# Order of TensorE's down-projections among the rounds of a pair of expert groups

## The chip, the cores and the metric

The kernel runs as one launch on one core of one Trainium2 chip. The metric is the device time in microseconds of that core, from launch to end; lower is better. The profile is one execution of the same program, recorded by the hardware. Its times count from the start of the span, the stretch from the core's first to its last instruction.

## The reference, cut to what matters

The whole program is a float32 transformer on 256 tokens of width 1024: two layers of one kind, then two of a second kind. The last layer ends in a mixture of experts, and only that part is touched here:

```
def moe_swiglu(x, w_router, w_gate, w_up, w_down):
    logits = (x @ w_router).astype(jnp.float32)
    top_val, top_idx = lax.top_k(logits, TOP_K)          # TOP_K = 2 of N_EXPERTS = 8
    top_w = jax.nn.softmax(top_val, axis=-1)
    gate = jnp.einsum('bsk,bske->bse', top_w, one_hot(top_idx, N_EXPERTS)).astype(x.dtype)
    y = jnp.zeros_like(x)
    for e in range(N_EXPERTS):
        h = jax.nn.silu(x @ w_gate[e]) * (x @ w_up[e])   # 1024 -> D_FF_EXPERT = 3584
        y = y + gate[..., e:e + 1] * (h @ w_down[e])     # 3584 -> 1024
    return y
```

Each expert has three weight matrices of 14.7 MB in float32, so the eight experts together have 352 MB that must come in from memory once.

## The kernel before, in words

**Which tokens.** For each expert the tokens that chose it are gathered into 96 slots (FIRST = 96, three tiles of 32). The function `first_slots` computes all eight experts for these slots; a later loop for experts with more than 96 tokens runs only if one has them.

**Groups and pairs.** The hidden width 3584 of an expert is cut in 7 groups of 512, so there are 56 groups in all, and `first_slots` takes them two at a time: 28 pairs, `q` = 0 to 27, with the groups `i0 = 2q` and `i1 = 2q + 1`, and a last turn `q` = 28 that only finishes. A group has three weight blocks of 2 MB: gate, up and down. The six blocks of a turn are loaded by SyncE (SP) in the order gate i0, up i0, down i0-2, gate i1, up i1, down i1-2, into a ring of six buffers. Load n may start when load n-6 is used, and SP waits for these one after the other in the order of the loads.

**Rounds.** The weights stream through TensorE (PE) while three 32-slot tiles of tokens are held, and four such 32-column tiles run side by side in the array. A pair has 2 groups x 2 matrices x 3 tiles = 12 products, which makes three rounds of four (`tiles`, L1248), 64 matmuls each. Round 1 writes a bank of ring "d" and is the last user of gate i0. Round 2 writes the other bank of "d", is the last user of up i0 and the first of gate i1. Round 3 writes a bank of ring "s" and is the last user of gate i1 and up i1.

**From rounds to the hidden values.** ScalarE (ACT) applies silu to the gate parts (L1633 to L1649) and VectorE (DVE) multiplies them by the up parts (L2265 to L2277). Rounds 1 and 2 give the half `hid_a`; round 3 gives the rest: ACT L1649, then DVE L2276 and L2277, which mark `hid_b`. Then PE turns the hidden values (`turn_hidden`): it waits for `hid_a`, makes four transposes (L1294), waits for `hid_b`, makes four more (L1300). ACT copies both to SBUF (L1656).

**Downs.** `down(i)` multiplies the turned hidden values of group i by its down block (48 matmuls, L1275 and L1281) and adds up over the 7 groups of the expert in two banks of ring "x". In turn q PE does the downs of the pair before, `i0-2` and `i1-2`. After an expert's seventh group ACT and DVE take the result away (`outcome`: ACT L1623, DVE L2232 to L2237), `scatter` spreads it back over the tokens (PE L1232, after round 1 of some turns) and DVE adds it up (`gather_out`, L2247). At three turns PE also gathers the tokens of two more experts (L1210) and turns their weights (L1221), both after round 2.

**What sets the order.** All of it is written out by hand, for each engine on its own: PE's loop at L1300 to L1331, ACT's at L1625 to L1658, DVE's at L2250 to L2281. Each engine executes in its own order, and an instruction that waits holds up everything behind it. The weights' order is set by the plan's loop over `gate_up` and `lower`.

Of the kernel before, what the change touches and what calls it, by code (L numbers as in the profile page):

```python
# [452 lines left out]
def build(nc, a, out, book, cut=None):  # L453
# [15 lines left out]
    with ExitStack() as ctx:  # L469
# [362 lines left out]
        def _(pe):  # L832
# [403 lines left out]
            def first_slots(groups):  # L1236

                per = len(groups) // EXPERTS
                x_of = [xs[i // per // 2 % 2][:, :, i // per % 2 * FIRST:(i // per % 2 + 1) * FIRST] for i in range(len(groups))]

                def tiles(r, parts, release):

                    views = {w: slot(w) for _, w, _ in parts}
                    b, n = bank(lane, r)
                    pe.wait_ge(*emptied(lane, r, n))
                    for k in range(KD):
                        for j, (i, w, c) in enumerate(parts):
                            last = pe.matmul(b[TILE * j:TILE * j + TILE, :], x_of[i][:, k, TILE * c:TILE * c + TILE],  # L1248
                                             views[w][:, k, :], start=(k == 0), stop=(k == KD - 1))
                    last.then_inc(*lane.tick(filled[r], ("full", r, n), *[("used", w) for w in release]))  # L1250

                accs = None

                def down(i):

                    nonlocal accs
                    at = i % per
                    if at == 0:
                        accs = [bank(lane, "x") for _ in range(2)]
                        for _, n in accs:  # L1260
                            pe.wait_ge(*emptied(lane, "x", n))
                    (b0, n0), (b1, n1) = accs
                    v = slot(groups[i]["down"])
                    pe.wait_ge(*lane.of(("hid_turned", i // 2)))

                    def mine(f, c):

                        turned, at = ((hid_a, (3, 0, 1)), (hid_b, (2, 3, 0)))[i % 2]
                        return turned[:, f, TILE * at[c]:TILE * at[c] + TILE]

                    for f in (0, 2):
                        first, final = at == 0 and f == 0, at == per - 1 and f == 2
                        for o in range(2):
                            for j, (c, half) in enumerate(((0, 0), (1, 0), (2, 0), (2, 1))):
                                last = pe.matmul(b0[TILE * j:TILE * j + TILE, :], mine(f + o, c),  # L1275
                                                 v[:, f + o, 512 * half:512 * half + 512], start=(first and o == 0),
                                                 stop=(final and o == 1))
                        if final:
                            last.then_inc(*lane.tick(x_full, ("full", "x", n0)))
                        for j, (c, o) in enumerate(((0, 0), (1, 0), (0, 1), (1, 1))):  # L1280
                            last = pe.matmul(b1[TILE * j:TILE * j + TILE, :], mine(f + o, c), v[:, f + o, 512:1024],  # L1281
                                             start=first, stop=final)
                    if at < per - 1:
                        last.then_inc(*lane.tick(down_done, ("e_down", i), ("used", groups[i]["down"])))
                    else:
                        last.then_inc(*lane.tick(x_full, ("full", "x", n1), ("e_down", i), ("used", groups[i]["down"])))

                def turn_hidden(q):

                    pe.wait_ge(*lane.of(("hid_a", q)))  # L1290
                    b, n = bank(lane, "a")
                    pe.wait_ge(*emptied(lane, "a", n))
                    for f in range(4):
                        last = pe.transpose(b[:, f * P:(f + 1) * P], hidden[:, 0, f * P:(f + 1) * P], ident[:, :])  # L1294
                    last.then_inc(*lane.tick(a_full, ("full", "a", n)))
                    pe.wait_ge(*lane.of(("hid_b", q)))
                    b, n = bank(lane, "a")
                    pe.wait_ge(*emptied(lane, "a", n))
                    for f in range(4):
                        last = pe.transpose(b[:, f * P:(f + 1) * P], hidden[:, 1, f * P:(f + 1) * P], ident[:, :])  # L1300
                    last.then_inc(*lane.tick(a_full, ("full", "a", n), ("hid_read", q)))

                gather(0)
                pairs = len(groups) // 2
                for q in range(pairs + 1):
                    i0, i1 = 2 * q, 2 * q + 1
                    if q < pairs:
                        g0, g1 = groups[i0], groups[i1]
                        pe.wait_ge(*lane.of(("xg", i0 // per // 2 * 2)))
                        tiles("d", [(i0, g0["gate"], 1), (i0, g0["gate"], 2), (i0, g0["gate"], 0), (i0, g0["up"], 0)],  # L1310
                              [g0["gate"]])
                    for m in scattered_at(q, per):
                        scatter(m)
                    if q < pairs:
                        pe.wait_ge(*lane.of(("xg", i1 // per // 2 * 2)))
                        tiles("d", [(i0, g0["up"], 1), (i0, g0["up"], 2), (i1, g1["gate"], 0), (i1, g1["gate"], 1)],
                              [g0["up"]])
                    for g in gathered_at(q, per):
                        gather(g)
                    for g in [0] if q == 0 else gathered_at(q, per):  # L1320
                        turn_weights(g)
                    if q:
                        down(i0 - 2)
                    if q < pairs:
                        tiles("s", [(i1, g1["up"], 2), (i1, g1["gate"], 2), (i1, g1["up"], 0), (i1, g1["up"], 1)],
                              [g1["gate"], g1["up"]])
                    if q:
                        down(i1 - 2)
                    if q < pairs:
                        turn_hidden(q)  # L1330
                scatter(EXPERTS - 1)  # L1331
                state["pass"], state["e_group"] = EXPERTS, len(groups)
# [122 lines left out]
        def _(act):  # L1455
# [169 lines left out]
            def first_slots(groups):  # L1625
# [3 lines left out]
                for q in range(pairs):  # L1629
# [3 lines left out]
                        act.wait_ge(*lane.of(("hid_b", q - 1)))  # L1633
                    act.activation(gated[96:P, 0, :], b[64:96, :], ACT.Silu).then_inc(*lane.tick(act_order, ("silu_0", q)))
                    act.activation(gated[0:64, 0, :], b[0:64, :], ACT.Silu).then_inc(*lane.tick(act_order))
                    b, n = bank(lane, "d")
                    act.wait_ge(*lane.of(("full", "d", n)))
                    act.activation(gated[64:P, 1, :], b[64:P, :], ACT.Silu).then_inc(*lane.tick(act_order, ("silu_1", q)))  # L1638
# [3 lines left out]
                        weights_turned(g)  # L1642
                    for _ in range(scattered_banks(q, per)):
                        bank(lane, "s")
                    if ended_at(2 * q - 2, per):
                        outcome((2 * q - 2) // per)
                    b, n = bank(lane, "s")
                    act.wait_ge(*lane.of(("full", "s", n)))
                    act.activation(gated[0:32, 1, :], b[32:64, :], ACT.Silu).then_inc(  # L1649
                        *lane.tick(act_order, ("silu_2", q)))  # L1650
                    if ended_at(2 * q - 1, per):
                        outcome((2 * q - 1) // per)
                    for dst in (hid_a, hid_b):
                        b, n = bank(lane, "a")
                        act.wait_ge(*lane.of(("full", "a", n)))
# [122 lines left out]
        def _(dve):  # L1778
# [471 lines left out]
            def first_slots(groups):  # L2250
# [3 lines left out]
                for q in range(pairs + 1):  # L2254
# [3 lines left out]
                    for g in gathered_at(q, per):  # L2258
                        picks(g)
                        weights(g)  # L2260
                    if q < pairs:
                        if q:
                            dve.wait_ge(*lane.of(("hid_read", q - 1)))
                        b, n = bank(lane, "d")
                        dve.wait_ge(*lane.of(("silu_1", q)))  # L2265
                        post(dve.tensor_tensor(hidden[96:P, 0, :], gated[96:P, 0, :], b[96:P, :], ALU.mult),  # L2266
                             ("free", "d", n), sem=d_free)
                        b, n = bank(lane, "d")
                        post(dve.tensor_tensor(hidden[0:64, 0, :], gated[0:64, 0, :], b[0:64, :], ALU.mult),
                             ("free", "d", n), ("hid_a", q), sem=d_free)  # L2270
                    if ended_at(i0 - 2, per):
                        outcome((i0 - 2) // per)
                    if q < pairs:
                        b, n = bank(lane, "s")
                        dve.wait_ge(*lane.of(("silu_2", q)))
                        post(dve.tensor_tensor(hidden[64:P, 1, :], gated[64:P, 1, :], b[64:P, :], ALU.mult))  # L2276
                        post(dve.tensor_tensor(hidden[0:32, 1, :], gated[0:32, 1, :], b[0:32, :], ALU.mult),  # L2277
                             ("free", "s", n), ("hid_b", q), ("e_hidden", i0), ("e_hidden", i1), sem=s_free)
                    if ended_at(i1 - 2, per):
                        outcome((i1 - 2) // per)  # L2280
                gather_out(EXPERTS - 1)  # L2281
                state["pass"], state["e_group"] = EXPERTS, len(groups)

# [148 lines left out]
```

## Time and profile before

| what | value |
|---|---|
| median of 3 runs | 2592.01 us (2587.98 to 2606.04) |
| the profiled execution | 2597.7 us |
| its span | 2595.8 us |
| TensorE busy | 2450.5 us, 94% of the span |
| VectorE, ScalarE busy | 485.5 us, 401.8 us |
| HBM read | 556.49 MB |

The profiled execution is 5.7 us longer than the median of the runs, and lies inside their range; 1.9 us of it lie around the span. In the page's strips one digit is a slice of 64.9 us. Busy times of different engines overlap and don't add up to the span. The tiles in the profile are named by the buffers that the kernel reuses: `hT` and `N` hold gathered tokens in this stage, `proj` holds the hidden values before and after ACT and DVE, `PT` the turned hidden values, `slots` the weight ring.

### The profile page before, as it was taken

Reading aid. Unit: us, or ns where it says so; the run is one execution under the profiler, and the core shown is the slowest. Engines: PE = TensorE matmul, PEld = TensorE weight load, DVE = VectorE, ACT = ScalarE, POOL = GpSimd, SP = SyncE. Lnnn points to the kernel's source line nnn. Section 1 sums busy time; section 2 is a strip of 40 time slices with the busy share of each in tenths; the row PEclk is TensorE's granted clock in tenths of the full one; section 3 lists DMA queues with packets and bytes.
Section 4 is the critical chain, followed back from the end, with each engine's and each line's share of the span. In section 5 each row is a group of like instructions: output and inputs, shape, how many; then the busy total and the mean of one; then the engine's idle time right before and its main releaser. Section 6 shows DMA issues by size and latency. Waiting matters only on the chain.

```text
span 2595.8 us, 33681 instructions
## 1 busy us (share of the span) xinstructions
PE 2450.5 (94%) x14810; PEld 1328.2 (51%) x14810; DVE 485.5 (19%) x1214; ACT 401.8 (15%) x970; POOL 109.0 (4%) x186
## 2 busy tenths in 40 slices
PE   7999999999999599999987897999999999999997
PEld 3678765578765264776647645333333333333332
DVE  3240003340001431200111623001011110111012
ACT  1330001330001151200010612110111111111101
POOL 2210100000000020000000200000000000000000
PEclk9899999999999779999995898999999999999999
DMA  9557634624333244243334223799999999999994
GB/s 291 182 54 184 222 114 141 219 86 151 130 122 131 96 138 148 105 158 133 134 98 146 74 102 120 264 391 373 358 369 390 373 357 370 392 336 370 390 372 165
DMA packets 247460, 567.89 MB, mean 219 GB/s; under 512 B 10224, under 2 KB 25776, under 8 KB 247312
## 3 DMA queue, kind: packets, MB, share of 16 engines
q1 hardware_dynamic: 235424, 532.24, 56.2%
q0 software_dynamic: 11888, 33.46, 5.9%
q8 instruction: 120, 1.97, 0.3%
q14 instruction: 28, 0.23, 0.0%
HBM read 556.49 MB, written 9.18 MB: 218 GB/s over the span
## 4 chain that ended last, share of the span: by engine, by line
PE 92%; DVE 4%; ACT 3%; issue 1%; DMA 1%; DVEq 0%; SPq 0%; ACTq 0%; POOLq 0%
PE ps_d L1248 15%; PE ps_a L874 12%; PE ps_x L1275 7%; PE ps_s L1248 7%; PE ps_a L1061 7%; PE ps_d L1061 7%; PE ps_x L1078 4%; PE ps_s L1078 4%; PE ps_x L1281 4%; PE ps_x L981 3%; PE ps_s L916 3%; PE ps_x L916 3%; PE ps_a L1045 2%; PE ps_a L963 2%; PE ps_d L1045 2%; PE ps_s L1232 1%
## 5 line engine op out<-in xcount | busy, mean ns | idle before, releaser
L874 PE MATMUL ps_a<-slots,hT 128*128 128x512 f32 (+4 forms) x672 | 275.2, 568 | 14.2 <-ACT hT L1485 9.9
L1275 PE MATMUL ps_x<-slots,PT 128*32 128x512 f32 x1792 | 212.9, 592 | 0.8 <-ACT PT L1656 0.8
L874 PEld LDWEIGHTS ps_a<-slots,hT 128*128 128x128 f32 x672 | 126.6, 195 | 156.0 <-issue 140.9
L1248 PE MATMUL ps_d<-slots,hT 128*32 128x512 f32 x1792 | 195.8, 593 | 0.6 <-ACT hT L1606 0.6
L1248 PE MATMUL ps_d<-slots,N 128*32 128x512 f32 x1792 | 196.0, 593 | 0.0
L1061 PE MATMUL ps_a<-hT,slots 128*128 128x256 f32 x864 | 192.7, 381 | 2.5 <-issue 2.5
L1061 PE MATMUL ps_d<-hT,slots 128*128 128x256 f32 x864 | 190.9, 379 | 0.0
L1061 PEld LDWEIGHTS ps_a<-hT,slots 128*128 128x128 f32 x864 | 165.0, 191 | 30.6 <-issue 8.5
L1061 PEld LDWEIGHTS ps_d<-hT,slots 128*128 128x128 f32 x864 | 164.2, 190 | 22.3
L2330 DVE TENSOR_TENSOR proj<-proj,ps_d 128x512 f32<-128x512 f32 x33 | 22.7, 688 | 597.7 <-PE ps_d L1061 523.7
L1275 PEld LDWEIGHTS ps_x<-slots,PT 128*32 128x32 f32 x1792 | 58.2, 110 | 132.9 <-issue 132.9
L1248 PEld LDWEIGHTS ps_d<-slots,hT 128*32 128x32 f32 x1792 | 56.4, 110 | 129.2 <-issue 128.4
L1248 PEld LDWEIGHTS ps_d<-slots,N 128*32 128x32 f32 x1792 | 56.3, 110 | 128.8 <-issue 128.8
L1078 PE MATMUL ps_x<-slots,proj 128*128 128x512 f32 x264 | 121.6, 592 | 0.0
L1078 PE MATMUL ps_s<-slots,proj 128*128 128x512 f32 x264 | 121.6, 592 | 0.0
L1281 PE MATMUL ps_x<-slots,PT 128*32 128x512 f32 x896 | 116.7, 592 | 0.0
L1600 ACT ACTIVATE proj<-ps_a 128x512 f32<-128x512 f32 x33 | 19.7, 597 | 543.6 <-PE ps_a L1061 516.0
L2266 DVE TENSOR_TENSOR proj<-proj,ps_d 32x512 f32<-32x512 f32 x28 | 19.4, 694 | 437.9 <-ACT proj L1638 437.9
L1248 PE MATMUL ps_s<-slots,hT 128*32 128x512 f32 x896 | 98.7, 592 | 0.0
L1248 PE MATMUL ps_s<-slots,N 128*32 128x512 f32 x896 | 98.7, 592 | 0.0
L1078 PEld LDWEIGHTS ps_x<-slots,proj 128*128 128x128 f32 x264 | 50.2, 190 | 63.1 <-issue 63.1
L1078 PEld LDWEIGHTS ps_s<-slots,proj 128*128 128x128 f32 x264 | 50.2, 190 | 56.7 <-issue 56.0
(346 smaller groups left out, 2362.7 us busy)
## 6 DMA issues: line engine op xcount, KB each, us to landing
slots<-in_moe_w_gate SPq DMA_DIRECT2D x56, 2048.0 KB, 9.8
slots<-in_moe_w_up SPq DMA_DIRECT2D x56, 2048.0 KB, 11.1
slots<-in_moe_w_down SPq DMA_DIRECT2D x56, 2048.0 KB, 12.0
slots<-in_ffn_w_gate_up SPq DMA_DIRECT2D x20, 2048.0 KB, 9.3
slots<-in_ffn_w_down SPq DMA_DIRECT2D x10, 2048.0 KB, 8.4
slots<-in_w_in SPq DMA_DIRECT2D x8, 2048.0 KB, 9.6
slots<-in_ff_w_gate SPq DMA_DIRECT2D x5, 2048.0 KB, 7.8
slots<-in_ff_w_up SPq DMA_DIRECT2D x5, 2048.0 KB, 7.7
```

The source lines that it names most:

```text
L874: last = pe.matmul(b[:, 0:c], lhs[:, k, t * P:(t + 1) * P], v[:, k, :], start=(k == 0), stop=(k == s["k"] - 1))
L916: last = pe.matmul(b[:, :], hT[:, k, t * P:(t + 1) * P], v[:, k, :], start=(k == ks[0]), stop=(k == ks[-1]))
L963: last = pe.transpose(b[:, at * P:(at + 1) * P], PR[:, u % 2, j, t, kc * P:(kc + 1) * P], ident[:, :])
L981: last = pe.matmul(b[:, o:o + dv], PT[:, u % 2, j, turned_at[kc, t], :], named[name][:, kc, c:c + dv], start=(kc == kcs[0]), stop=(kc == k ...
L1045: last = pe.matmul(b[:, f * S + t * P:f * S + (t + 1) * P], v[:, k, (f0 + f) * P:(f0 + f + 1) * P], hT[:, k, t * P:(t + 1) * P], start=(k ...
L1061: last = pe.matmul(b[:, f * S:(f + 1) * S], v[:, k, (f0 + f) * P:(f0 + f + 1) * P], hT[:, k, :], start=(k == 0), stop=(k == KD - 1))
L1078: last = pe.matmul(b[:, :], hid[:, n_group % 2, f, t * P:(t + 1) * P], v[:, f, half * 512:(half + 1) * 512], start=start, stop=stop)
L1232: pe.matmul(b[:, :], gives[:, m // 2 % 2, m % 2, t * P:(t + 1) * P], y_e[0:FIRST, 512 * half:512 * half + 512], start=True, stop=True).the ...
L1248: last = pe.matmul(b[TILE * j:TILE * j + TILE, :], x_of[i][:, k, TILE * c:TILE * c + TILE], views[w][:, k, :], start=(k == 0), stop=(k == ...
L1275: last = pe.matmul(b0[TILE * j:TILE * j + TILE, :], mine(f + o, c), v[:, f + o, 512 * half:512 * half + 512], start=(first and o == 0), st ...
L1281: last = pe.matmul(b1[TILE * j:TILE * j + TILE, :], mine(f + o, c), v[:, f + o, 512:1024], start=first, stop=final)
L2330: dve.tensor_tensor(hid[:, n_group % 2, f0:f0 + 2, :].rearrange("p f s -> p (f s)"), silu[:, p % 2, :], b[:, :], ALU.mult).then_inc(*lane. ...
```

## The change

Within a turn PE's order is changed. Written without the scatters and gathers, it was

```
round 1, round 2, down(i0-2), round 3, down(i1-2), turn_hidden
```

and it becomes

```
round 1, down(i0-2), round 2, down(i1-2), round 3, turn_hidden
```

ACT and DVE take away an expert's result (`outcome`) correspondingly earlier in their own order. The order of the loads is not changed, nor is any instruction's shape.

```diff
@@ PE, first_slots
                     for m in scattered_at(q, per):
                         scatter(m)
+                    if q:
+                        down(i0 - 2)
                     if q < pairs:
                         ...
                     for g in [0] if q == 0 else gathered_at(q, per):
                         turn_weights(g)
                     if q:
-                        down(i0 - 2)
+                        down(i1 - 2)
                     if q < pairs:
                         tiles("s", [(i1, g1["up"], 2), (i1, g1["gate"], 2), (i1, g1["up"], 0), (i1, g1["up"], 1)],
                               [g1["gate"], g1["up"]])
-                    if q:
-                        down(i1 - 2)
                     if q < pairs:
                         turn_hidden(q)
@@ ACT, first_slots
                     act.activation(gated[0:64, 0, :], b[0:64, :], ACT.Silu).then_inc(*lane.tick(act_order))
+                    if ended_at(2 * q - 2, per):
+                        outcome((2 * q - 2) // per)
                     b, n = bank(lane, "d")
                     ...
-                    if ended_at(2 * q - 2, per):
-                        outcome((2 * q - 2) // per)
+                    if ended_at(2 * q - 1, per):
+                        outcome((2 * q - 1) // per)
                     b, n = bank(lane, "s")
                     act.wait_ge(*lane.of(("full", "s", n)))
                     act.activation(gated[0:32, 1, :], b[32:64, :], ACT.Silu).then_inc(
                         *lane.tick(act_order, ("silu_2", q)))
-                    if ended_at(2 * q - 1, per):
-                        outcome((2 * q - 1) // per)
@@ DVE, first_slots
+                    if ended_at(i0 - 2, per):
+                        outcome((i0 - 2) // per)
                     if q < pairs:
                         ...
-                    if ended_at(i0 - 2, per):
-                        outcome((i0 - 2) // per)
+                    if ended_at(i1 - 2, per):
+                        outcome((i1 - 2) // per)
                     if q < pairs:
                         b, n = bank(lane, "s")
                         ...
-                    if ended_at(i1 - 2, per):
-                        outcome((i1 - 2) // per)
```

## Rows read from the trace of the kernel before

**Rows 1.** The page: busy by engine; strips of PE's clock and of DMA.
```profile
PE 2450.5 (94%) x14810; PEld 1328.2 (51%) x14810; DVE 485.5 (19%) x1214; ACT 401.8 (15%) x970; POOL 109.0 (4%) x186
...
PEclk9899999999999779999995898999999999999999
DMA  9557634624333244243334223799999999999994
```

**Rows 2.** Groups of PE in 1653.4:2560: busy, mean ns, idle before.
```profile
L1275 PE MATMUL ps_x<-slots,PT 128*32 128x512 f32 x1600 | 190.0, 592 | 0.0
...
L1300 PE MATMUL ps_a<-ident,proj 128*128 128x128 f32 x102 | 15.4, 273 | 0.0
```

**Rows 3.** Timeline of PE, turn q = 4: start, us, work, xcount.
```profile
1749.66 13.94 PE L1248 MATMUL ps_d<-slots,hT 128*32 128x512 f32 x128
1763.42 1.90 PE L1275 MATMUL ps_x<-slots,PT 128*32 128x512 f32 x16
...
1768.57 7.05 PE L1248 MATMUL ps_s<-slots,hT 128*32 128x512 f32 x64
1775.43 1.90 PE L1275 MATMUL ps_x<-slots,PT 128*32 128x512 f32 x16
...
1780.70 0.65 PE L1294 MATMUL ps_a<-ident,proj 128*128 128x128 f32 x4
...
1781.72 7.07 PE L1248 MATMUL ps_d<-slots,hT 128*32 128x512 f32 x64
```

**Rows 4.** Timeline of all engines at the end of turn q = 0.
```profile
1643.67 7.07 PE L1248 MATMUL ps_s<-slots,hT 128*32 128x512 f32 x64
...
1650.68 0.65 PE L1294 MATMUL ps_a<-ident,proj 128*128 128x128 f32 x4
...
1650.81 0.59 ACT L1649 ACTIVATE proj<-ps_s 32x512 f32<-32x512 f32 x1 [6.37 <-PE ps_s L1248]
...
1651.43 0.69 DVE L2276 TENSOR_TENSOR proj<-proj,ps_s 64x512 f32<-64x512 f32 x1 [6.07 <-ACT proj L1649]
1652.16 0.68 DVE L2277 TENSOR_TENSOR proj<-proj,ps_s 32x512 f32<-32x512 f32 x1
...
1652.89 0.66 PE L1300 MATMUL ps_a<-ident,proj 128*128 128x128 f32 x4 [1.56 <-DVE proj L2277]
1653.47 1.92 PE L1248 MATMUL ps_d<-slots,hT 128*32 128x512 f32 x16
```

**Rows 5.** Waits in 1660:2580: us in total, times, longest.
```profile
ACT proj L1649 <- PE ps_s L1248: 288.3, 27, 11.6
...
PEld ps_s L1232 <- DVE O L2247: 9.9, 15, 0.8
```

**Rows 6.** Timeline of SP (weight loads) in turn q = 4.
```profile
1743.62 0.37 SPq L660 DMA_DIRECT2D slots<-in_moe_w_gate  x1
...
1768.81 0.37 SPq L660 DMA_DIRECT2D slots<-in_moe_w_down  x1
```

**Rows 7.** DMA issues in 1743:1749: KB, us from issue to landing.
```profile
slots<-in_moe_w_gate SPq DMA_DIRECT2D x1, 2048.0 KB, 10.1
...
slots<-in_moe_w_down SPq DMA_DIRECT2D x1, 2048.0 KB, 15.5
```

**Rows 8.** The same in 1756:1769, of three loads the last.
```profile
slots<-in_moe_w_down SPq DMA_DIRECT2D x1, 2048.0 KB, 11.3
```

**Rows 9.** The same in 1599:1601, with no other load on the way.
```profile
slots<-in_moe_w_gate SPq DMA_DIRECT2D x1, 2048.0 KB, 7.9
```

**Rows 10.** Window with the pause of turn q = 0: length, busy (PE, PEld, DVE, ACT, POOL), clock, DMA.
```profile
1650.00:1660.00 10.00, 8.44 (x80) 2.88 (x76) 1.37 (x2) 1.78 (x3) 0.00 (x0) 1.00 0.85 311
```

**Rows 11.** Windows after a wait of 5.44 us of PE, before the experts.
```profile
1622.00:1624.00 2.00, 2.00 (x8) 2.00 (x7) 0.00 (x0) 0.00 (x0) 0.00 (x0) 0.50 0.04 8
1624.00:1626.00 2.00, 2.00 (x11) 2.00 (x10) 0.00 (x0) 0.49 (x1) 0.00 (x0) 0.74 0.00 0
```

**Rows 12.** Timeline of PE there: the gather of the first two experts.
```profile
1621.45 7.20 PE L1210 MATMUL ps_a<-proj,X 128*128 128x192 f32 x32 [5.44 <-DVE O L2204]
```

## The prediction, made before the change was run

> **What bounds the kernel now.** I read four views, from coarse to fine. The page first: TensorE (PE) is busy for 94% of the span, and in the last 14 slices, where the experts lie, it runs at a clock of 9 tenths or more while the DMA strip shows nines too [rows 1]. So two resources are near full there. The groups of PE over the experts say which one sets the pace: from 1653.4 to 2560 us not one group has idle time before it, the transposes L1300 and the downs L1275 included [rows 2]. Nothing PE waits for comes late. What is gained on another engine, or by an earlier transfer, is worth nothing here; the only thing that can change the time is a gap between PE's instructions.
>
> The timeline of one turn gives the parts [rows 3]. Rounds 1 and 2 start at 1749.66 and the first down at 1763.42, so a round is 6.88 us; the next starts give down 5.15 (1763.42 to 1768.57) and round 3 6.86 (1768.57 to 1775.43). The turn ends when the next one's round 1 starts, at 1781.72: 32.06 us. I use 6.87 for a round. From the start of the second down (1775.43 + 5.15 = 1780.58) to the next turn there are 1.14 us, the two sets of transposes with a small gap ahead of them.
>
> **What the second down does there now.** It stands between round 3 and the transposes, and round 3's results need time: ACT must apply silu, DVE must multiply twice, and only then may PE do L1300. The first turn, q = 0, has no downs, so it is exactly the end of a turn that the change makes everywhere: round 3, then the transposes at once. There the chain is bare [rows 4]: round 3 starts at 1643.67, the first transposes at 1650.68, ACT at 1650.81, DVE at 1651.43 and 1652.16, and L1300 at 1652.89 after 1.56 us of idle PE, released by DVE L2277. The next round 1 starts at 1653.47, 9.80 us after round 3 began.
>
> **The sum, part by part.**
> - Down i0-2 moves ahead of round 2. It needs `hid_turned` of the turn before, which ACT copies out after L1300, about 0.6 us a copy by the like of ACT L1649 [rows 4]; round 1 with 6.87 us still lies between. Nothing for its wait. Without round 1 ahead of it the wait would show, but that is so in turn 28 alone, before and after alike.
> - Down i1-2 moves ahead of round 3. Both moves leave 48 matmuls of 5.15 us as they are, and rows 3 show no gap at the borders of round and down (starts 6.87 and 5.15 apart). Nothing for the move itself.
> - The end of a turn. Before: round 3, down, 1.14, so 6.87 + 5.15 + 1.14 = 13.16 us (1768.57 to 1781.72). After: down 5.15, then the pattern of q = 0 with 9.80, so 14.95 us. The difference is **1.79 us** per turn. Turns with downs and transposes are q = 1 to 27; ACT L1649 and PE met 27 times in this view [rows 5]. 27 x 1.79 = **48.3 us**. From below, the idle time alone, 1.56, would give 42.1 us. From above, if L1294 were not hidden in the wait either (it lasts 0.65 with its tail, 0.5 by the starts), 2.28 would give 61.6 us. I take 1.79, since it is the measured distance of the same instructions in the same order at the same clock.
> - Can ACT or DVE be late for this chain? Both idle until round 3 ends: ACT L1649 waited 288.3 us in 27 times on PE, 10.7 us each [rows 5]. Their new work ahead of it, `outcome`, now belongs to a down that ended a whole round (6.87 us) before. Four short instructions of about 0.7 us each fit in it. Nothing.
> - The banks of ring "x". When an expert ends on i0-2, down i1-2 starts the next expert and must find both banks empty. Round 3 covered that before, round 2 does now, with the same 6.87 us. Nothing; bare, it would be those same 2.8 us, four times.
> - Scatters stay after round 1 and gathers after round 2, with the same neighbours ahead. Scatter's short waits on DVE, 9.9 us in 15 times [rows 5], stay.
> - The loads. SP's queue is passed in the old order, but the buffers come free in another one. Count from the start of round 1. Before: gate i0 at 6.87, up i0 13.74, down 18.9, gate i1 and up i1 25.8, down 30.9. After: gate i0 6.87, up i0 and the down (freed earlier, but behind it in SP's order) 18.9, and gate i1, up i1 and the second down all at 30.9. What does a load take? From the landing of the gate issued at 1743.62 (+10.1 = 1753.7) to that of the down issued at 1768.81 (+11.3 = 1780.1) five more loads land in 26.4 us, 5.28 each; alone, a load takes 7.9 [rows 6 to 9], so 2.6 us pass before its bytes flow. After: three loads issued at 30.9 land at 38.8, 44.1 and 49.3. They are needed one turn (33.85 us) later: gate i1 at 45.9, up i1 at 57.9, the down at 52.7. The next gate i0 and up i0 land at 54.6 and 60.5 and are needed at 67.7, the first down at 65.8 for 74.6. The smallest reserve is **3.4 us**, of down i1-2. Before it was about 2.8, of gate i1 (landed 1753.7, needed at 1749.66 + 6.87 = 1756.5), and no wait came of it. The six loads fill 31.7 us of a turn that is now 33.85. Nothing, as a reserve of that size held before.
>
> The sum: 2597.7 + 48.3 = 2646.0 us for an execution like the profiled one, whose span would be 2644. The median of the runs lies 5.7 us under the profiled execution, so I forecast 2592.0 + 48.3 = **2640 us**, 1.9% slower. There is no term on the other side, since PE had no idle time to win back.
>
> **The clock.** In the window with the pause of q = 0 PE was busy 8.44 of 10 us and the granted clock was 1.00, that is 2.4 GHz [rows 10]. The new pauses are of that size, one per 33.85 us. The Trainium skill (TensorE: Matmul & The Clock Gate, section "A second HAM failure mode: psum-queue depth-cycling") says that short idle times between groups of matmuls, when frequent, can make the clock swing between its two levels. The one pause here speaks against it; 27 in a row have not been seen.
>
> **The rivals.**
> 1. *The clock falls at each pause* (chance 0.05). After a wait of 5.44 us the first gather began at 1621.45 [rows 12], at a granted clock of 0.50; the window 1624 to 1626 has 0.74, about the middle [rows 11], so some 3.5 us ran at 1.2 GHz, of which half, 1.8 us, is lost. At all 27 pauses: 47 us more, 2687 us. For it: many pauses, and ring banks in turn; against: rows 10.
> 2. *Weights come late* (0.06). Three loads now leave together, and the last has three services ahead of its need. It decides once that load takes over 21.8 us from issue instead of the 18.4 worked out; the longest of rows 7 is 15.5, with two in front of it. Every microsecond over that stalls PE before round 3's down, in 27 turns: at one over, 2667 us. In PE's waits L1275 would then stand behind a DMA.
> 3. *Not slower: the chain hides* (0.05). If L1300 finds `hid_b` ready sooner than in q = 0, say because ACT and DVE answer round 3 faster in the steady turns, the pause shrinks. The point at which it decides is 0.96 us per turn (26 / 27): below it the change is within 1%. At no pause at all and with scatter's waits gone too, which now meet other neighbours, the time is 2592.0 - 9.9 = 2582 us; with the pause at half, 2616 us. Against it: ACT started 0.13 us after PE's next instruction and DVE 0.03 us after ACT ended in q = 0 [rows 4], so nothing in the chain but work is left.
> 4. *The change does not do what it says* (0.02): a wait hidden in semaphore values keeps PE's order in effect, 2592 us. PE executes in its written order, so this is nearly excluded.
>
> The forecast itself has the remaining 0.82. Its own range is 2592 + 42 = 2634 to 2592 + 62 = 2654, and medians of three runs here spread by some microseconds (runs from 2588 to 2606), so 2628 to 2658. Reaching a little into rivals 2 and 3 gives 2622 to 2662, which leaves out less than 2 in 10. A measurement of this kernel tells about 1% (26 us) from no change. Slower by over 1%: forecast, rivals 1 and 2, 0.93, less a little for a pause near 1 us, 0.91. Within 1%: 0.08. Faster by over 1%: 0.01, as nothing idle is there to be won.
>
> **What would show it.** PE's group L1300 with about 42 us of idle before it in 27 to 28 waits, each near 1.56, released by DVE L2277; starts of round 1 33.85 us apart in plain turns; the ACT wait for round 3 unchanged in kind; down groups L1275 with no idle; a clock of 1.00 from 1700 on; DMA at a mean some 5% lower over the experts (31.7 of 33.85). It would be wrong if L1275 or L1248 wait for a DMA (rival 2), if the clock strip shows less than nines (rival 1), or if L1300's idle is well under 26 us in all (rival 3).

## The result, and the profile after

The changed kernel takes 2646.97 us in the median of 4 runs (2633.74 to 2660.04), the kernel before 2599.03 us in its 4 (2587.98 to 2611.62). The ratio is 1.0183, with a 95% interval of 1.0095 to 1.027. In a second set, 6 runs against 17, it is 1.0194 (1.0153 to 1.0235). The change makes the kernel slower by 1.8 to 1.9%; 1.9% was forecast.

Single executions of either kernel differ by 25 us, half of the effect, so I measure the part that the change touches by itself: from the start of the first gather (L1210) to the start of the last scatter (L1232), called "the stage" below. In the kernel before it began at 1621.45 [rows 12]. Its end in the kernel before, in the timeline of PE:

```profile
2577.64 3.86 PE L1232 MATMUL ps_s<-proj,PR 96*128 96x512 f32 x8 [1.49 <-issue]
```

Both ends in the changed kernel, in the same view:

```profile
1609.47 2.90 PE L1210 MATMUL ps_a<-proj,X 128*128 128x192 f32 x8 [5.44 <-DVE O L2204]
...
2613.69 3.86 PE L1232 MATMUL ps_s<-proj,PR 96*128 96x512 f32 x8 [1.49 <-issue]
```

The stage takes 956.2 us before and 1004.2 after: **48.0 us more**, where 48.3 were worked out. Two lines of the page of the changed kernel answer to [rows 1]; the clock is at nines in the experts' slices as before, and PE has lost a little of its share:

```profile
PE 2445.6 (93%) x14810; PEld 1318.3 (50%) x14810; DVE 484.2 (18%) x1214; ACT 403.9 (15%) x970; POOL 108.8 (4%) x186
...
PEclk9999999999999699999976998999999999999999
```

Where the idle time is, the groups of PE over the experts say (1653.4:2590; columns as in [rows 2]):

```profile
L1275 PE MATMUL ps_x<-slots,PT 128*32 128x512 f32 x1696 | 201.6, 593 | 0.0
...
L1300 PE MATMUL ps_a<-ident,proj 128*128 128x128 f32 x104 | 17.1, 287 | 40.4 <-DVE proj L2279 40.4
```

One group alone has any, L1300, and its releaser is DVE L2279, the multiply that was L2277 [rows 2, 4]. The window leaves out the pause of turn 0 and that of turn 27, so these are 26 of the 28. The DMA share over 1700 to 2500 us has a mean of 0.95 in windows of 100 us, where it was 1.00, the 5% less that was named as a sign. One turn in the timeline of PE (against [rows 3]):

```profile
1733.44 7.05 PE L1248 MATMUL ps_s<-slots,hT 128*32 128x512 f32 x64
1740.42 0.66 PE L1294 MATMUL ps_a<-ident,proj 128*128 128x128 f32 x4
1742.63 0.66 PE L1300 MATMUL ps_a<-ident,proj 128*128 128x128 f32 x4 [1.55 <-DVE proj L2279]
1743.22 7.07 PE L1248 MATMUL ps_d<-slots,hT 128*32 128x512 f32 x64
1750.11 1.90 PE L1275 MATMUL ps_x<-slots,PT 128*32 128x512 f32 x16
...
1762.12 1.90 PE L1275 MATMUL ps_x<-slots,PT 128*32 128x512 f32 x16
```

Round 3 to the next round 1 is 9.78 us (turn 0 had 9.80), and the next round 1 starts at 1777.05, 33.83 us after this one's 1743.22, against 32.06 before. In the chain of waits one such pause reads, in order of time (start, us, what):

```profile
1706.72 0.60 ACT proj L1651
1707.32 0.02 issue
1707.35 0.69 DVE proj L2278
1708.04 0.03 issue
1708.07 0.69 DVE proj L2279
1708.76 0.04 issue
1708.80 0.66 PE ps_a L1300 x4
```

Round 3's last matmul is done at 1706.70. Silu and two multiplies, 2.0 us of work with 0.1 us between them: there is nothing in the chain but work. In every turn with rounds the end has become what the end of turn 0 was [rows 4].

### The profile page after: what moved, and what is told of

Same layout as the page of the kernel before. It is cut to its first block, busy times and chain, and to the rows that moved or that the text cites. A ratio compares the mean times of both kernels' runs of the same rounds, so it can differ in the third digit from the quotient of the medians.

```text
span 2631.9 us, 33681 instructions
## 1 busy us (share of the span) xinstructions
PE 2445.6 (93%) x14810; PEld 1318.3 (50%) x14810; DVE 484.2 (18%) x1214; ACT 403.9 (15%) x970; POOL 108.8 (4%) x186
## 4 chain that ended last, share of the span: by engine, by line
PE 90%; DVE 5%; ACT 3%; issue 1%; DMA 1%; DVEq 0%; SPq 0%; ACTq 0%; POOLq 0%
PE ps_d L1248 15%; PE ps_a L874 12%; PE ps_x L1275 7%; PE ps_s L1248 7%; PE ps_a L1061 7%; PE ps_d L1061 7%; PE ps_x L1078 4%; PE ps_s L1078 4%; PE ps_x L1281 4%; PE ps_x L981 3%; PE ps_s L916 3%; PE ps_x L916 3%; PE ps_a L1045 2%; PE ps_d L1045 2%; PE ps_a L963 2%
```

## The experiments

In every table "stage" is first gather to last scatter in the profiled execution, and the ratio is to the kernel before, with its 95% interval. The changed kernel's two profiles agree within 0.2 us in the stage, which is what makes effects of a few microseconds readable at all.

| kernel | stage, us | ratio |
|---|---|---|
| before | 956.2 | 1 |
| changed | 1004.2 | 1.0183 (1.0095 to 1.027) |
| after_again: changed, once more | 1004.0 | 1.0194 (1.0153 to 1.0235) |
| first_down_only | 956.4 | 1.0011 (0.9982 to 1.0041) |
| second_down_only | 1011.5 | 1.0216 (1.0172 to 1.0259) |
| turn_b_late | 988.8 | 1.0131 (1.0089 to 1.0172) |
| shorter_chain | 986.6 | 1.0126 (1.0070 to 1.0182) |
| longer_chain | 1041.2 | 1.0313 (1.0257 to 1.0369) |
| slightly_longer | 1023.5 | 1.0275 (1.0231 to 1.0318) |
| longer_chain_before | 956.9 | 1.0006 (0.9976 to 1.0037) |
| after_loads | 1004.0 | 1.0176 (1.0133 to 1.0219) |
| turn_b_later | 963.6 | 1.0036 (1.0005 to 1.0067) |
| turn_b_later_loads | 963.4 | 1.0043 (1.0017 to 1.0069) |

**The same kernel again.**

> The changed kernel once more, timed in more rounds. From its first gather to its last scatter it took 1004.2 us, the kernel before 956.2 us. Bare chain at the end of a turn: the expert stage is again 1004 us within 1 us, some 48 us over before, ratio near 1.018. Late weights: the stage may vary by several us between executions, since memory does. Clock falling at the pauses: a granted clock under 1.00 in some windows of the experts, and a stage that varies. Any difference between executions that all three leave over must lie ahead of the experts.

The stage is 1004.0 us. The span of this execution was 2656.7 us, 24.8 more than in the profile above, and all of it lies ahead of the stage: its first gather starts at 1634.5 instead of 1609.5. The last section says what it is.

**Each move alone.** The first move by itself:

```diff
 round 1
+down(i0 - 2)
 round 2
-down(i0 - 2)
 round 3
 down(i1 - 2)
 turn_hidden(q)
```

> Only the first move: round 1, down i0-2, round 2, round 3, down i1-2, transposes. Bare chain: the second down stands between round 3 and the transposes again, so the whole loss goes: stage 956 us, the time of before, ratio 1.000 within 0.4%; PE's L1300 idle in turn 0 alone, 1.6 us. Late weights: the buffers of up i0 and down i0-2 still come free together, only gate i1, up i1 and down i1-2 don't, so a part of the loss stays if loads in bunches are its cause (10 to 30 us). Clock: no pauses, no loss.

The stage is 956.4 us, the time of before. PE's waits in it are those of before, the pause of turn 0 and two at the very end (engine, line, releaser, us in total, times, longest):

```profile
PE ps_a L1300 <- DVE proj L2277: 1.6, 1, 1.6
PE ps_s L1232 <- issue: 1.5, 1, 1.5
PE ps_x L1275 <- ACT PT L1656: 0.8, 1, 0.8
```

The second move by itself:

```diff
 round 1
 round 2
 down(i0 - 2)
+down(i1 - 2)
 round 3
-down(i1 - 2)
 turn_hidden(q)
```

> Only the second move: round 1, round 2, down i0-2, down i1-2, round 3, transposes. Bare chain: the 48 us are all there, since nothing stands between round 3 and the transposes. And a second price shows four times (turns 4, 11, 18, 25, where an expert ends on down i0-2): down i1-2 must now wait until the result of the last expert has left both banks, some 2 to 2.8 us each, 8 to 11 us in all. So a stage of about 1013 us, ratio 1.021. Late weights: the three loads at the end of a turn leave together as in the changed kernel, so about 1004 as well; only the waits in the profile, on DVE and not on a DMA, tell that apart.

1011.5 us. The pauses belong to the second move. And the second price is there, in the waits of PE (1640 to 2610 us, which leaves out the 28th pause):

```profile
PE ps_a L1300 <- DVE proj L2278: 41.9, 27, 1.6
PE ps_x L1275 <- DVE proj L2236: 6.0, 4, 1.5
```

L2236 is the last step of `outcome`. It came up 4 times and the stage is 1011.5 - 1004.2 = 7.3 us longer, 1.8 each, a little under the 8 to 11 expected. In the changed kernel round 2 stands there, and PE's waits have no such line.

**The chain covered, all else as changed.** The transposes of hid_b move behind the next round 1:

```diff
 round 1
+turn_b(q - 1)        # L1300's transposes and ACT's copy
 down(i0 - 2)
 round 2
 down(i1 - 2)
 round 3
-turn_hidden(q)
+turn_a(q)            # L1294's transposes and ACT's copy
```

> The changed order, but the second set of transposes (of hid_b, L1300) and its copy on ScalarE are put behind round 1 of the next turn. Rounds, downs and all releases of weights stay in the changed order, in bunches. Bare chain: 6.9 us of round 1 cover it, the pauses go, and the stage is back at 956 to 961 us (up to 0.15 us per turn more for one more border between transposes and matmuls), ratio 1.000 to 1.002. Late weights: the bunches stay and a turn has less time, so if they cost the 48 us, the stage stays near 1004 and L1275 or L1248 wait for a DMA. Clock: no pauses, no loss.

This missed: 988.8 us, not 956 to 961. The old pause is gone, and there is a new one, again bare, because the down waits for ACT's copy of what has just been turned (in the seven turns that are not counted a scatter stands between):

```profile
PE ps_x L1275 <- ACT PT L1638: 26.9, 21, 1.3
```

I had counted the cover of the first link, transposes after multiply, and not of the next, down after copy. Here no DMA is among the waits either, though the releases of the weights are in bunches as in the changed kernel. The next version puts a down between:

```diff
 round 1
+down(i0 - 2)         # waits for hid_a's copy only
 turn_b(q - 1)
-down(i0 - 2)
 round 2
 down(i1 - 2)         # waits for hid_b's copy
```

> The changed order with the transposes of hid_b behind down i0-2 of the next turn, which needs hid_a alone; down i0-2 waits for hid_a's copy only, down i1-2 for hid_b's. Round 1 and the down cover the chain to the transposes, round 2 covers ScalarE's copy, which stood bare (1.3 us, 20 to 21 times) when the transposes came right before the down. Bare chain: no pause is left, a stage of 956 to 960 us, ratio 1.000 to 1.003. Late weights: a turn has only some 32.2 us now and the load of down i1-2 landed 19.8 us after the end of round 3, while it is needed after 0.6 + 6.9 + 5.15 + 0.6 + 6.9 = 20.1 us. This rival is alive here for the first time: some turns may wait for a DMA at L1275, 0 to 0.5 us each, up to 10 us.

963.6 us: of the 48.0 us, 40.6 are gone. What is left is in the timeline of PE for one turn:

```profile
1698.55 7.05 PE L1248 MATMUL ps_s<-slots,hT 128*32 128x512 f32 x64
1705.53 0.66 PE L1294 MATMUL ps_a<-ident,proj 128*128 128x128 f32 x4
1706.12 7.07 PE L1248 MATMUL ps_d<-slots,hT 128*32 128x512 f32 x64
...
1718.27 0.66 PE L1303 MATMUL ps_a<-ident,proj 128*128 128x128 f32 x4
1718.86 7.07 PE L1248 MATMUL ps_d<-slots,hT 128*32 128x512 f32 x64
```

Each set of four transposes now costs 0.59 us and 0.11 us at its border (1705.53 less 1698.55 is 6.98, not 6.87). That is 1.40 us for both sets, where the two side by side took 1.14. The whole turn is some 32.35 us, 0.29 more than 32.06. 27 x 0.29 = 7.8, less 1.6 of turn 0, plus 0.8 for a second wait at the end, are 7.0 of the 7.4 us that are left. The 0.12 to 0.15 us that my expectations allow for the border was too small. PEld also showed a wait for weights, of which the next section tells.

**Late weights.** The changed kernel with the loads in the order in which the buffers come free:

```diff
-gate i0, up i0, down i0-2, gate i1, up i1, down i1-2
+gate i0, down i0-2, up i0, down i1-2, gate i1, up i1
```

> The changed kernel with the six loads of a turn in the order in which its buffers come free: gate i0, down i0-2, up i0, down i1-2, gate i1, up i1. No three loads leave together any more, and every block lands at least 5 us ahead of its use. Bare chain: the time is that of the changed kernel, stage 1004 us, ratio 1.018 to 1.019, pauses of L1300 unchanged. Late weights: were the bunched loads the cause of any of the 48 us, that part comes back and the stage is shorter than 1004.

1004.0 us, with PE pausing ahead of L1303 (the line that is L1300 elsewhere) for 43.5 us in 28 times. The order of the loads has no part in the loss. Yet the reserve in the changed kernel was thinner than I had worked out. The three loads that leave together, in the timeline of SP, and what they took from issue to landing (window 1735:1745 of the DMA view):

```profile
1740.55 0.37 SPq L660 DMA_DIRECT2D slots<-in_moe_w_gate  x1
1740.96 0.58 SPq L660 DMA_DIRECT2D slots<-in_moe_w_up  x1
1741.59 3.94 SPq L660 DMA_DIRECT2D slots<-in_moe_w_down  x1
```
```profile
slots<-in_moe_w_gate SPq DMA_DIRECT2D x1, 2048.0 KB, 9.2
slots<-in_moe_w_up SPq DMA_DIRECT2D x1, 2048.0 KB, 14.2
slots<-in_moe_w_down SPq DMA_DIRECT2D x1, 2048.0 KB, 18.7
```

The third landed at 1741.59 + 18.7 = 1760.3 and was needed at 1762.12: 1.8 us of reserve where 3.4 were forecast. In the split version, whose turn is shorter, this became a wait of PEld, the weight loads of PE (first fence), and with the new load order it went (second fence, all that PEld waits for there but issue):

```profile
PEld ps_x L1275 <- DMA slots<-in_moe_w_down: 5.3, 12, 0.6
```
```profile
PEld ps_s L1235 <- DVE O L2261: 10.5, 16, 0.8
```

> The split transposes (hid_b's behind down i0-2 of the next turn) together with the load order of the buffers' release. In the split version alone the stage was 963.6 us: 956.2, and 5.3 us in 12 waits for the down weights, and about 27 x 0.12 us for one more border between transposes and matmuls, less 1.6 us of turn 0. Late weights explain the 5.3 us and no more: with the new load order they go, and the stage is 958 to 959 us. If those waits had another cause they stay. The ratio to the kernel before is then 1.002, or 1.000 where ours can't be told apart.

The wait went, and the time did not: 963.4 us against 963.6. So those 5.3 us had cost nothing that shows. They stand in PEld's table and not in PE's: the load of the next weights waited up to 0.6 us while the matmuls before it still ran. The sum that gave them 5 us was wrong, and the borders above take that place.

**The length of the chain.** VectorE's first multiply of round 3 reads only what the silu of round 2 wrote, so it need not wait for `silu_2`, the silu of round 3:

```diff
-dve.wait_ge(*lane.of(("silu_2", q)))
+dve.wait_ge(*lane.of(("full", "s", n)))
 post(dve.tensor_tensor(hidden[64:P, 1, :], gated[64:P, 1, :], b[64:P, :], ALU.mult))
+dve.wait_ge(*lane.of(("silu_2", q)))
 post(dve.tensor_tensor(hidden[0:32, 1, :], ...
```

> The changed kernel, but VectorE's first multiply of round 3, which does not read what ScalarE's silu L1651 writes, waits for round 3 alone and not for that silu; only the second multiply waits for it. Silu (0.59 us) and first multiply (0.69) then run side by side. Bare chain: it is shorter by about 0.6 us in each of 28 turns, 15 to 18 us less than the changed kernel, a stage of about 987 to 989 us, ratio near 1.012. If the two engines hinder each other at the same bank, less is won. Late weights: down i1-2 had 1.6 to 2.1 us of reserve in the changed kernel, so its weights could just begin to be late; by that rival nothing is won.

986.6 us, 17.6 less than the changed kernel, 0.63 us per turn. The timeline shows silu and multiply starting together and the pause down from 1.55 to 0.93 us; both engines at one bank did not slow either:

```profile
1704.09 0.59 ACT L1651 ACTIVATE proj<-ps_s 32x512 f32<-32x512 f32 x1 [11.42 <-PE ps_s L1248]
1704.09 0.69 DVE L2278 TENSOR_TENSOR proj<-proj,ps_s 64x512 f32<-64x512 f32 x1 [9.92 <-PE ps_s L1248]
...
1705.54 0.66 PE L1300 MATMUL ps_a<-ident,proj 128*128 128x128 f32 x4 [0.93 <-DVE proj L2280]
```

The other way, with that multiply done twice:

```diff
 post(dve.tensor_tensor(hidden[64:P, 1, :], gated[64:P, 1, :], b[64:P, :], ALU.mult))
+dve.wait_ge(*lane.own())
+post(dve.tensor_tensor(hidden[64:P, 1, :], gated[64:P, 1, :], b[64:P, :], ALU.mult))
```

> The changed kernel with VectorE's first multiply of round 3 (64x512, 0.69 us) done twice, the second time after waiting for the first: the chain from round 3 to the transposes L1300 is longer by one such instruction and a wait. Bare chain: every added nanosecond shows in each of the 28 turns, 0.69 to 0.75 us x 28 = 19 to 21 us over the changed kernel, so a stage (first gather to last scatter) of 1024 us against 1004.2, and L1300's mean pause 2.3 us instead of 1.55. Late weights or a clock that falls: VectorE's work doesn't enter, no more than 1 or 2 us; a longer pause would even give the weights more time.

1041.2 us, 37.0 more than the changed kernel, nearly twice what every theory of mine said. The pause itself grew as it should, from 43.5 to 63.8 us in 28 times, 20.3 us. The rest is the clock. The windows around the end of one such pause, at 1722.67 (columns as in [rows 10]), and the group of rounds 1 and 2 in one half of the experts:

```profile
1722.00:1724.00 2.00, 1.33 (x12) 0.71 (x16) 0.61 (x1) 0.60 (x1) 0.00 (x0) 1.00 1.04 401
1724.00:1726.00 2.00, 2.00 (x15) 0.47 (x11) 0.00 (x0) 0.00 (x0) 0.00 (x0) 0.50 1.05 403
1726.00:1728.00 2.00, 2.00 (x19) 0.55 (x15) 0.00 (x0) 0.00 (x0) 0.00 (x0) 0.64 1.05 387
1728.00:1730.00 2.00, 2.00 (x24) 0.64 (x20) 0.00 (x0) 0.00 (x0) 0.00 (x0) 1.00 1.05 387
```
```profile
L1248 PE MATMUL ps_d<-slots,N 128*32 128x512 f32 x1792 | 205.6, 613 | 0.0
```

The granted clock is 0.50 soon after the pause and 1.00 again by 1728; the group's mean is 613 ns where it was 593 in the changed kernel. By the starts of the matmuls, 9 of the 27 rounds 1 that follow a pause are longer, eight by 1.70 us and one by 1.15, with 0.45 more in the transposes just ahead of it. The down that follows the 28th pause is longer by 1.70 too. Together 16.9 us, which with the 20.3 makes 37.2, 0.2 over the 37.0: the first gather was that much shorter. Is there a pause in between at which this begins? A repeat of 192 instead of 512 columns:

> The changed kernel with a small repeat of VectorE's first multiply (64x192, about 0.3 us) in the chain, between the changed kernel (pause 1.55 us, stage 1004 us, clock 1.00) and the one with the whole repeat (pause 2.27 us, stage 1041 us). The whole repeat cost 37 us: 20 us of pause and some 17 us in which the granted clock was at 0.5 after a pause. By pause alone this one costs 28 x 0.35 = 10 us, stage 1014 us, clock 1.00 among the experts. If the clock falls after pauses of 1.9 us too, the stage is longer by up to another 17 us and round 1's matmuls have a mean above 593 ns.

1023.5 us, 19.3 more than the changed kernel, with pauses of 1.94 us. After 5 of the 28 pauses the clock fell: 4 rounds 1 are longer, and the down behind the last pause. One of the rounds, in the timeline of PE, takes 8.77 us instead of 7.07 (first fence). The down's first 16 matmuls take 2.85 us, where they take 1.92 in the changed kernel (second and third fence):

```profile
1976.75 0.66 PE L1300 MATMUL ps_a<-ident,proj 128*128 128x128 f32 x4 [1.94 <-DVE proj L2281]
1977.33 8.77 PE L1248 MATMUL ps_d<-slots,N 128*32 128x512 f32 x64
```
```profile
2632.73 2.85 PE L1275 MATMUL ps_x<-slots,PT 128*32 128x512 f32 x16 [0.78 <-ACT PT L1656]
```
```profile
2601.69 1.92 PE L1275 MATMUL ps_x<-slots,PT 128*32 128x512 f32 x16 [0.78 <-ACT PT L1656]
```

Five times 1.7 are 8.5 us, and 28 x 0.39 us of longer pause are 10.9, together the 19.3 within 0.1. At pauses of 1.55 us, in the changed kernel, its repetition and the one with the other load order, no round 1 of 81 is longer, nor is the down behind the last pause. What makes the clock fall at one pause and not at the next was not tested, and each of the longer chains was profiled once.

**The control: the longer chain in the old order.** The same doubled multiply in the kernel before:

> The kernel before with the same doubled multiply (0.69 us and a wait) in VectorE's part of round 3. Bare chain: here down i1-2 (5.15 us) covers the chain, which grows from 2.1 to 2.8 us, so only turn 0, which has no down, is longer: stage 956.2 + 0.7 = 956.9 us, ratio 1.000. If VectorE's work cost time in another way (SBUF or PSUM traffic beside TensorE), the stage would grow by up to 20 us as well.

956.9 us: 0.7 more, all of it in turn 0. The instruction that cost 37.0 us in the one order costs 0.7 in the other.

## Why the prediction was right

- *No idle time of PE to win.* Right: first_down_only, which changes nothing but the place of one down and its `outcome`, neither wins nor loses anything (956.4 against 956.2 us).
- *1.79 us per turn, 48.3 us in all, from turn 0's bare chain.* Right to 0.3 us: 48.0 in the stage, 1.77 by the turns' starts (33.83 less 32.06). That it is this chain is shown from both sides: 0.63 us off it moves the stage by 28 times as much, 0.73 us on it lengthens the pauses 28 times, and the same instruction in the old order, where the down stands between round 3 and the transposes, costs once.
- *Nothing for the moves themselves, for ACT and DVE, and for the x banks.* Right. The cover of the x banks was real: without it, second_down_only paid 7.3 us. I had priced it bare at 2.8 us each; it was 1.8.
- *Rival 2, late weights.* Rightly small, but its distance was mis-sized: 1.8 us of reserve, not 3.4. I let the three loads leave at the end of round 3 in one instant and took 18.4 us for the third. SP issued the first 0.24 us after the end of round 3 and the third 1.04 us after the first, and that one took 18.7. Nor would a lateness of a few tenths have cost what I gave it, as the split version showed.
- *Rival 1, the falling clock.* It did not come at 1.55 us, where the profile shows 1.00 throughout. But 0.05 was a guess from one pause, and the kernel stood nearer to it than I knew: 0.4 us more of pause and it began. The Trainium skill's warning (TensorE: Matmul & The Clock Gate, section "A second HAM failure mode: psum-queue depth-cycling") against frequent short idle times is borne out by the two kernels with longer pauses (15 falls in 56 pauses), not by the changed one. The price per fall, 1.8 us from [rows 11], came out at 1.70. That was in part luck: I took those rows for a clock that a wait of 5.44 us had brought down, and it was down before that wait began at 1616, as this window of the kernel before shows:

```profile
1612.00:1616.00 4.00, 2.26 (x10) 2.21 (x10) 1.73 (x11) 1.24 (x2) 0.00 (x0) 0.50 0.84 274
```

- *Rival 3, the chain hides.* Wrong in each of its parts: the steady turns had turn 0's pause to 0.01 us, and scatter's short waits stayed (10.5 us in 16 times over the stage, before and after). Nor were these waits PE's time to win back, as I priced them: they stand in the table of PEld [rows 5], and none of PE's own waits is on DVE L2247.
- *The span of 2644 us.* The profiled execution had 2631.9. The 12 us lie ahead of the stage, in code that the change does not touch (last section). For the same reason the median came to 2647 us where 2640 was forecast: the four runs are two near 2634 and two near 2660, and the kernel before had 2599 in the same set, not 2592. That the difference of the medians, 47.9 us, is that close to 48.3 is luck; the 48.0 of the stage is not.

No version beats the kernel before. The split transposes come to 0.4% of it and stay slower, mostly by their borders; the old order, with the second down as cover, has no gap to fill but turn 0's 1.6 us.

## What to carry to other kernels

Where one engine is busy without a gap, as PE was here, the order of its work is worth what it covers: before moving an instruction, ask which chain on other engines runs behind it, and look for a turn (the first, the last) in which it is missing already; that turn has the price. Count the cover link by link, for the result of a covered step may be waited for at once. And a pause can cost more than its length: here the clock never fell after 1.55 us and did after some of those of 1.94 us, so a chain that is bare should at least be short.

## What the runs showed of the hardware

**The clock after a pause.** TensorE's granted clock stayed at 1.00 (2.4 GHz) after 84 pauses of 1.55 us (28 in each of three executions), fell to 0.50 (1.2 GHz) after 5 of 28 of 1.94 us and after 10 of 28 of 2.28 us, in a stream that was otherwise dense. Each fall cost 1.6 to 1.7 us. All 15 falls came within 2.3 us of the end of a pause. Whether it falls at a given pause did not follow from the kernel: neighbours with the same work differ.

**Two executions of the same kernel, 25 us apart.** The first attention stage is the same code before and after. In the kernel before, two windows of it (first fence), in the changed one the same two (second):

```profile
110.00:120.00 10.00, 10.00 (x48) 8.84 (x46) 2.18 (x12) 5.14 (x15) 0.00 (x0) 0.50 0.07 27
120.00:130.00 10.00, 10.00 (x47) 9.04 (x47) 2.39 (x10) 2.81 (x10) 0.00 (x0) 0.50 0.01 2
```
```profile
110.00:120.00 10.00, 10.00 (x88) 9.01 (x87) 5.51 (x26) 8.18 (x28) 0.00 (x0) 1.00 0.26 100
120.00:130.00 10.00, 10.00 (x87) 8.89 (x87) 3.38 (x6) 7.72 (x24) 0.00 (x0) 1.00 0.00 0
```

With PE marked busy in both, one execution did 95 matmuls in these 20 us and the other 175. By the starts of VectorE's instructions the two executions are within 2 us of each other up to 108 us and 11.3 us apart from 134 us on. The repeated run of the changed kernel lost 12 us at this place as well and 13 more in the attention of the second layer, where its windows from 510 to 530 us have a clock of 0.50, and those of the first profile 1.00:

```profile
510.00:520.00 10.00, 10.00 (x47) 8.38 (x44) 2.46 (x13) 4.89 (x17) 0.00 (x0) 0.50 0.31 108
```
```profile
510.00:520.00 10.00, 10.00 (x83) 8.85 (x82) 3.38 (x6) 8.32 (x26) 0.00 (x0) 1.00 0.01 2
```

In these three executions one stage not at full clock costs 12 us, two cost 25. The other ten profiles sort the same way: the stage of the experts begins at 1608 to 1613 us where the clock was at 1.00 in both places, at 1621 to 1628 where it was low in one, and at 1637 where it was low in both. So single runs spread over 25 us while the stage of the experts repeats within 0.2. What decides whether the clock is up stays open.
